# Attention in the order scores, transpositions, value products; own block of the paired sample units with a depth of 128 rows

## The reference, cut to what matters

```
s = einsum('bqhd,bkhd->bhqk', qi, k) * scale          # scores of a block of 128 queries
if has_bias: s = s + bias_q - bias_k                  # FoX only
p = softmax(where(visible, s, -inf), axis=-1)         # over the keys
return einsum('bhqk,bkhd->bqhd', p, v)                # value products
# MLA: k_nope = ckv_all @ w_uk, v = ckv_all @ w_uv, k = [k_nope, shared rotary key]
```

## Time and profile before

| | |
|---|---|
| timed runs | 1239.88, 1240.25, 1240.64 us; median 1240.25 us |
| the profiled execution's own time | 1235.15 us |
| its span, first to last instruction | 1233.1 us |
| PE busy | 1119.4 us, 91% of the span |
| DVE, ACT, POOL busy | 559.4, 254.0, 222.4 us |
| mean granted TensorE clock | 0.97 of full speed |
| FoX attention stage | from 308.8 to 361.4 us |
| MLA group 1, group 2 | from 772.1 to 829.9 us, from 864.1 to 923.3 us |

### The profile page before, as it was taken

One profiled execution on the slowest core, in us unless ns is written; L12 is line 12 of the kernel. 1 busy time (PEld: TensorE's weight loads), 2 busy tenths in 40 slices (PEclk: granted clock), 3 DMA queues, 4 the chain that ended last, 5 costly groups with the idle time before them and its releaser, 6 DMA issues.

```text
span 1233.1 us, 18806 instructions
## 1 busy us (share of the span) xinstructions
PE 1119.4 (91%) x7327; PEld 623.0 (51%) x7332; DVE 559.4 (45%) x1346; ACT 254.0 (21%) x610; POOL 222.4 (18%) x382
## 2 busy tenths in 40 slices
PE   8999999999889979999949989999999988999965
PEld 4556777554664633333315546776774553333312
DVE  2079879610643353744357140440442354554336
ACT  1214245321420000111101122332320000111112
POOL 0106445420201110101044210000000111100114
PEclk9999999999899989999989999999999989999987
DMA  8103302261734186999766222001205175899835
GB/s 355 69 9 141 125 33 105 86 226 65 44 130 175 52 345 246 339 413 375 281 214 222 70 106 69 1 1 68 69 8 231 62 298 209 329 397 407 316 103 196
DMA packets 41974, 215.54 MB, mean 175 GB/s; under 512 B 4504, under 2 KB 6104, under 8 KB 32544
## 3 DMA queue, kind: packets, MB, share of 16 engines
q1 hardware_dynamic: 24432, 153.28, 31.8%
q0 software_dynamic: 17168, 60.27, 15.8%
q10 hardware_dynamic: 288, 0.80, 0.2%
HBM read 181.02 MB, written 33.29 MB: 174 GB/s over the span
## 4 chain that ended last, share of the span: by engine, by line
PE 78%; DVE 9%; issue 4%; DMA 3%; ACT 3%; POOL 1%; DVEq 0%; SPq 0%; ACTq 0%
PE pair L1516 12%; PE pair L1131 9%; PE pair L1410 9%; PE pair L1537 7%; PE pair L1252 5%; PE pair L1330 5%; PE pair L1614 5%; PE pair L1142 4%; PE pair L1374 3%; PE pair L1119 2%; PE pair L1502 2%; PE pair L1372 2%; DMA ring<-in_even_w_in 2%; DMA arena<-x_rows,ints 1%; PE pair L1647 1%
## 5 line engine op out<-in xcount | busy, mean ns | idle before, releaser
L1516 PE MATMUL pair<-ring,arena 128*32 128x512 f32 x608 | 128.5, 595 | 0.0
L1131 PE MATMUL pair<-ring,xT 128*128 128x512 f32 x256 | 111.3, 593 | 0.9 <-DMA ring<-in_even_w_in 0.9
L1516 PE MATMUL pair<-arena 128*32 128x512 f32 x736 | 100.5, 600 | 8.0 <-issue 4.5
L1252 PE MATMUL pair<-xT,ring 128*128 128x296 f32 x320 | 85.1, 421 | 6.9 <-ACT arena L1726 3.0
L883 POOL TENSOR_SCALAR small<-small 128x1 f32<-128x1 f32 (+3 forms) x45 | 15.2, 337 | 386.9 <-DVE small L2264 334.5
L905 POOL TENSOR_TENSOR arena<-arena 128x128 f32<-128x128 f32 x140 | 58.4, 451 | 145.5 <-PE pair L1178 78.9
L1131 PEld LDWEIGHTS pair<-ring,xT 128*128 128x128 f32 x256 | 48.1, 190 | 59.7 <-issue 57.9
L1330 PE MATMUL pair<-arena 128*128 128x264 f32 (+8 forms) x270 | 74.6, 407 | 2.8 <-ACT arena L1716 1.8
L1031 POOL DMA_INDIRECT arena<-x_rows,ints x26 | 26.4, 1014 | 264.9 <-PE pair L1502 163.4
L1252 PEld LDWEIGHTS pair<-xT,ring 128*128 128x128 f32 x320 | 60.4, 193 | 25.8 <-issue 9.3
L2402 DVE COPY arena<-pair 128x256 f32<-128x256 f32 x26 | 11.0, 423 | 135.4 <-PE pair L1525 135.4
(11 more groups left out here) (385 smaller groups left out, 1968.1 us busy)
## 6 DMA issues: line engine op xcount, KB each, us to landing
arena<-in_moe_w_gate_up SPq DMA_DIRECT2D x14, 2048.0 KB, 8.8
ring<-in_moe_w_gate_up SPq DMA_DIRECT2D x12, 2048.0 KB, 9.4
arena<-in_moe_w_down SPq DMA_DIRECT2D x14, 1024.0 KB, 9.2
y_rows<-arena SPq DMA_DIRECT2D x26, 512.0 KB, 8.5
ring<-in_moe_w_down SPq DMA_DIRECT2D x12, 1024.0 KB, 11.3
xT<-in_moe_w_gate_up SPq DMA_DIRECT2D x6, 2048.0 KB, 14.6
ring<-in_even_w_in SPq DMA_DIRECT2D x5, 2048.0 KB, 7.9
y_rows<-xr POOLq DMA_DIRECT2D x12, 512.0 KB, 8.5
```

What stands on the lines that cost most here:

```text
L1131: last = pe.matmul(ps[0:P, 0:n], xT[:, k, 128 * i:128 * i + P], w[:, k, :], start=(k == 0), stop=(k == chunks - 1))
L1252: last = pe.matmul(ps[0:w.shape[2], 512 * s:512 * s + n], w[:, k, :], xT[:, k, n * s:n * s + n], start=(k == 0), stop=(k == KD - 1))
L1516: last = pe.matmul(bank[c, :], xgT[:, e % 2, k, c], expert_place(x)[0][:, k, :], start=(k == 0), stop=(k == KD - 1))
```

## The change

Three edits.

1. In `attention` of PE, transpose(n-2) stands ahead of values(n-3). In `attention` of DVE, the round is max(n), scale(n-1), own(n-2), out(n-3). ACT's round is as it was. The same functions serve the FoX stage and both MLA groups.
2. The own block of a pair unit has 128 rows in place of 64: `own_keys` gives columns 16 to 143 of the probabilities (the last 64 of them belong to cached keys) and rows 0 to 127 of the transposed block. So the own transposition has 128 columns out of the probabilities in place of 64, its copy by DVE 128 rows, and the own value product a depth of 128.
3. The rows for that product come from `cvp`, a new buffer of 256 columns: rows 0 to 63 are a copy of `cvo`, rows 64 to 127 are zero, so that the additional 64 probabilities add nothing. DVE fills it once, ahead of the MLA groups.

```diff
         qrm = r3.take(MH * NM)
+        cvp = r3.take(KVL)
...
             if kind == "pair":
-                return slice(NM, 80), slice(0, NS)
+                return slice(NM, NM + 128), slice(0, 128)
...
-                    values = [(cvo[rows, 128 * c:128 * c + 128], [ckpv[:, j, 128 * c:128 * c + 128] for j in range(nb)])
+                    own = cvp if kind == "pair" else cvo
+                    values = [(own[rows, 128 * c:128 * c + 128], [ckpv[:, j, 128 * c:128 * c + 128] for j in range(nb)])
                               for c in range(2)]
...
                     if n < last:
                         att_scores(n)
+                    if first <= n - 2 < last:
+                        att_transpose(n - 2)
                     if n - 3 >= first:
                         att_values(n - 3)
-                    if first <= n - 2 < last:
-                        att_transpose(n - 2)
...
                     if n < last:
                         att_max(n)
+                    if first <= n - 1 < last:
+                        att_scale(n - 1)
+                    if first <= n - 2 < last:
+                        att_own(n - 2)
                     if n - 3 >= first:
                         att_out(n - 3)
-                    if first <= n - 2 < last:
-                        att_own(n - 2)
-                    if first <= n - 1 < last:
-                        att_scale(n - 1)
...
             dve.memset(qrm, 0.0).then_inc(pez_sb.sem, 1)
+            dve.memset(cvp[NS:128, :], 0.0)
+            copy(cvp[0:NS, :], cvo[0:NS, :])
```

## The result

| | before | after |
|---|---|---|
| timed runs, median | 1240.45 us | 1227.32 us |
| ratio, with 95% interval | | 0.9893 (0.9868 to 0.9917) |
| the profiled execution's own time | 1235.15 us | 1226.22 us |
| its span | 1233.1 us | 1223.3 us |

The kernel is faster by 13.3 us by the ratio (10.3 to 16.4), where 6.9 were forecast. The sign and the mechanism were right, the size was not.

The account below looks back on a forecast made before the run. PE was taken to bound the kernel, with gaps from waits in the attention stages. Terms -1.4 - 1.0 - 2.0 + 0.5 - 3.0 = -6.9 us gave 1233.3 from 1240.25; range 1230.0 to 1238.3 for 8 in 10.

Parts of the forecast that it names:

- The waits for L1869 go: Running heads: value products no longer wait for ACT's copy of transposed blocks; gaps of 1.7 us a FoX head.
- The PSUM pair is late next: FoX heads: transpositions then wait for DVE's copy freeing the pair, 1.42 us a head in place of 1.7.
- the length of DVE's round: 592-key round: 2.62 us from scores' end to PE's restart against 1.37 of PE work, a wait of 1.25.
- running heads of FoX: Inside the FoX stage: each head 0.35 us shorter, 1.4 us for four.
- end of FoX: Last three FoX rounds, without scores as cover: from 8.3 to 7.2 us, taken as 1.0 less.
- inside the groups: MLA groups ahead of their ends: waits of 4.0 us become 4.5, so 0.5 us lost.
- ends of the groups: Ends of both MLA groups: from 7.5 to 6.6 us, taken as 1.0 less each, 2.0 in all.
- depth: MLA pair units: 128 rows remove the excess at 64-row passes, 0.74 us in each of four units, 3.0 us.
- Given back later: Rival, 0.12: stages behind attention take 5 of 7 us back, about 1238.5; the forecast itself gave 0, -2 to +2.
- The waits only change hands: Rival, 0.15: the new order gives nothing and the depth all, -3.0 us, 1237.2.
- The depth does nothing: Rival, 0.07: 128 rows in MLA pair units save nothing, leaving -3.9 us, 1236.4.
- The scaling blocks the freeing copy: Rival, 0.06: DVE's scaling, awaiting a late exponential, delays the PSUM pair; at 0.2 us a unit +4.5, 1244.8.

Follow-up runs that it names:

- e2: The kernel before with edit 1 alone, the new order on PE and DVE, pair units kept at 64 rows; -7.9 us (-11.0 to -4.8) against before.
- e1: The kernel before with edits 2 and 3 alone, the depth of 128 in the old order; -3.3 us (-6.0 to -0.6) against before.
- e5: The changed kernel plus two unread DVE memsets in every round, between scaling and own copy; -2.9 us (-5.6 to -0.1) against before.
- e9: The changed kernel with key blocks transposed ahead of the own block and ACT's copy ahead of its exponential; -19.1 us (-22.3 to -15.9) against before.
- e10: e9 with DVE's scaling also ahead of its maximum in the MLA groups; -21.6 us (-23.6 to -19.5) against before.

## Why the prediction was wrong in size

**What bounds the kernel** was right: PE's chain, and waits of PE in each stage.

**The waits for L1869 go**: right, and none is left at the stage ends either. **The PSUM pair is late next**: right, L1348 waits for L2214, longest in the 592-key round. It doesn't wait for L2194 in running heads (in the first head it does, 1.8 us, as the stage fills).

**The failed step is the length of DVE's round.** I added up whole rows: 0.97 + 0.68 + 0.29 + 0.29 = 2.23, and 2.62 with the ways to and from PE. In after it is 328.99 - 327.03 = 1.96, and from the scores' end (326.61 + 0.21) to the transposition 329.14 - 326.82 = 2.32. The trace of before had this already, and I did not use it. Its DVE rows around those of the earlier trace rows:

```profile
342.82 0.15 DVE L2191 RECIPROCAL small<-small 128x1 f32<-128x1 f32 x1
...
343.42 0.30 DVE L2180 CUSTOM_DVE_ANT_0 arena<-pair,arena 128x144 f32<-128x144 f32 x1
```

Reciprocal and scaling hold DVE 343.42 - 342.82 = 0.60 us, not 0.68, and the own copy 342.82 - 342.61 = 0.21, not 0.29. I read PE's work by the starts and DVE's by the rows' durations. In a round where PE waits, 0.3 us of length is 0.3 us of wait. The terms that hang on such waits hold about 3.0 of the 5.1 us by which the stages gained more than forecast. Another 1.4 lie in the first head, by the clock, and 0.8 are a term that I had put at nothing in the groups, the masks (below). By term:

| term | forecast | measured | |
|---|---|---|---|
| running heads of FoX | -0.35 each | -0.75, -0.59, -0.49 (heads 2, 3, 4) | the forecast waits of 0.42, 0.83 and 0.17 us, 1.42 a head, are 0.11, 0.76 and 0.12, together 1.0 |
| first head | -0.35 | -1.78 | about 1.5 of it the clock |
| end of FoX | -1.0 | -1.3 | |
| ends of the groups | -2.0 | -2.4 | 1.2 in each |
| inside the groups | +0.5 | -1.8 | the rest of e2's -4.2 (2.04 + 2.12) |
| depth | -3.0 | -2.8 | e1 |

The largest miss is inside the groups. I expected waits of 0.8 to 1.0 us in five or six places; after has three in group 1, from the end of the mask to the start of the transposition 0.48, 0.48 and 0.66. The round with a pair unit runs from 795.57 (scores' end) to 797.67, 2.1 us and not 2.4, and PE's work in it covers 1.6. The wait after subtraction is a difference of two near numbers, so 0.3 us of error changed it by a third or more, and turned the sign of the term. e5 shows the same slope from the other side.

The waits are about two thirds of that miss. Laid mask by mask over e1, which has the old order and the same depth, group 1 of after is 0.94 us shorter ahead of its last mask: 0.53 in the three rounds that wait, and 0.42 in the nine others that have value products, 0.04 to 0.05 each. There the work right behind the mask has changed. Before, and then after:

```profile
777.96 0.47 PE L1372 MATMUL pair<-arena 128*128 128x128 f32 x2
778.27 0.39 PE L1374 MATMUL pair<-arena 128*128 128x128 f32 x2
...
775.57 0.31 PE L1348 MATMUL pair<-cst,rb 128*128 128x128 f32 x1
775.71 0.38 PE L1350 MATMUL pair<-cst,rb 128*128 128x128 f32 x2
```

Behind a short mask two value passes take 0.31 us in place of 0.22, a transposition 0.14 in place of 0.11. The forecast had 0.03 for this in FoX and left it out of the groups.

**Depth** was right. The excess was at the 64-row passes and went nearly whole (0.70 of 0.74 us a unit): two own passes cost 0.42 us with 64 rows and 0.22 with 128, in e1 as in after. In e1 the two outputs are still in one bank, and on PE only the own transposition's width and the place of the own rows differ besides. A small row count alone doesn't cost this: in before, two passes with weights of 80 rows take 336.86 - 336.63 = 0.23 us, while four of 16 rows, in the meta unit, take 913.70 - 913.06 = 0.64 in place of 0.44. So the excess is 0.2 us for a group of two such passes and for one of four.

The Trainium skill, "TensorE: Matmul & The Clock Gate", Step-by-step, says that the row count doesn't matter to a weight load. The trace agrees as far as the loads go (PEld shows 0.29 us for the two of 64 rows at 790.01, 0.30 for two of 128 rows in after), but a term of 0 doesn't follow from it, since the excess lies outside them. The Trainium skill, "TensorEngine Tiling (Array Packing)", Key Properties, says that a change of tiling mode drains the engine. That fits the excess, but no run here tells it from another cost of the passes with few rows.

**Given back later: 0** is borne out by the timed runs, as far as their 3 us either way tell: stages -12.05 (about -10.6 with the clock's 1.5 left out), timed -13.3. The profiled pair alone would have misled, since 2.6 us of the gain were lost between FoX and group 1, where the same products took 5.6 us more of PE at a mean clock of 0.96 against 0.97.

**The rivals.** "The waits only change hands" falls by e2 (-7.9). "The depth does nothing" falls by e1. "The scaling blocks the freeing copy" falls: in after neither reciprocal nor scaling waits for its exponential in a running head. The closest is that of the 592 keys, whose exponential ends at 328.90 with its row sum; DVE comes to the reciprocal at 329.32, 0.4 us later. The range was too narrow on the fast side, since it left no room for an error in the reading of DVE's rows.

## What to carry to other kernels

Where one engine waits for another's round, take the round's length from starts, not from the durations of its rows; in a trace in which nobody waits for that round's end no wait will correct you. An order written out for several engines has to be changed on all of them at once: here PE's alone cost 7 us beyond the depth's gain, DVE's alone gave nothing, both gave 8. After such a change read what is late next and ask which part of the late step needs the wait: letting one transposition of up to five wait in place of all took another 5.5 us from the stages (2 in the timed medians, whose intervals overlap), and ACT's copy ahead of its exponential 1.7 more.

## What the runs showed of the hardware

- Two passes with weights of 64 rows among passes of 128 cost 0.42 us in place of 0.22; a unit with two such places cost 0.70 us more (e1). Four passes of 16 rows cost 0.64 in place of 0.44; two of 80 rows cost 0.23 (before).
- A DVE row can outlast the start of the next one, by about 0.08 us: 0.49 and 0.41 for a scaling of 128 x 528, 0.28 and 0.20 for a copy of 128 x 128 out of PSUM (after). A memset of 128 x 192 that waited for the one in front of it started 0.33 us after it, 0.11 behind the end of its row of 0.22; the next copy started 0.13 us after the second memset (e5).
- PE started a transposition 0.15 us after the row of the DVE copy that it waited for had ended (328.99 and 329.14; 331.09 and 331.24, after); DVE started 0.21 us after the end of the scores (326.82 and 327.03).
- The granted clock at one place of the program differs between executions of kernels whose code is the same there: over the first head 1.00 in e9 and 0.66 in e10, which took 8.12 and 9.96 us.
